# A chunked RWKV-7 scan on TensorE: products with a shared loaded side move 128 columns, k, b and v are turned by VectorE and GpSimd

## What is computed

```python
def rwkv7_scan(r, w, k, v, a, b):
    def step(state, inp):
        r_t, w_t, k_t, v_t, a_t, b_t = inp
        sa = jnp.einsum('bhvk,bhk->bhv', state, a_t)
        state = state * w_t[:, :, None, :] + sa[..., None] * b_t[:, :, None, :] + v_t[..., None] * k_t[:, :, None, :]
        return state, jnp.einsum('bhvk,bhk->bhv', state, r_t)
```

## Time and profile before

| | us |
|---|---|
| median of 3 runs | 2076.54 (2075.88 to 2079.14) |
| the profiled execution | 2082.89 |
| its span | 2081.1 |
| the scan in it, first to last matmul of L2650 | 734.8 to about 931.8 |

### The profile page before, as it was taken

The page is one execution under the profiler, slowest core; times in us unless marked ns, Lnnn a source line. Parts: engine busy times, 40 slices in busy tenths (PEclk is TensorE's granted clock), DMA queues, the critical chain, the costliest instruction groups (busy, mean ns, idle before and its releaser), DMA issues.

```text
span 2081.1 us, 34844 instructions
## 1 busy us (share of the span) xinstructions
PE 1975.6 (95%) x14762; PEld 1523.2 (73%) x14762; DVE 1091.2 (52%) x1727; ACT 802.3 (39%) x1363; POOL 378.3 (18%) x431
## 2 busy tenths in 40 slices
PE   8989999999999977669999999999999999999999
PEld 6847888888766666655887765468887778888887
DVE  4364444444667744437454765544455446666432
ACT  4264323232546522224324456654244442322211
POOL 0551000000303442212200036622221010000000
PEclk9999999999999999999999999999999999999999
DMA  5203333333342210001366210023332233333232
GB/s 184 78 26 96 91 101 91 91 94 98 102 152 73 81 44 4 5 6 67 96 167 216 70 33 1 1 93 101 91 115 80 70 95 97 91 92 96 89 94 86
DMA packets 46747, 174.87 MB, mean 84 GB/s; under 512 B 5072, under 2 KB 5584, under 8 KB 45825
## 3 DMA queue, kind: packets, MB, share of 16 engines
q1 hardware_dynamic: 43488, 154.09, 24.4%
q0 software_dynamic: 3104, 18.56, 2.7%
HBM read 166.26 MB, written 10.55 MB: 85 GB/s over the span
## 4 chain that ended last, share of the span: by engine, by line
PE 90%; issue 3%; DVE 3%; ACT 3%; POOL 0%; DMA 0%; SPq 0%; DVEq 0%; ACTq 0%; POOLq 0%
PE ps L300 22%; PE ps L301 22%; PE ps L305 22%; PE ps L2650 6%; PE ps L1425 2%; PE ps L1012 2%; PE ps L1409 1%; PE ps L1689 1%; ACT arena L1520 1%; PE ps L1378 1%; DVE arena L1481 1%; DVE arena L1465 1%; PE ps L1846 1%; PE ps L3228 1%; PE ps L2054 1%
## 5 line engine op out<-in xcount | busy, mean ns | idle before, releaser
L280 ACT ACTIVATE w_hi<-wring 128x1024 fp32r<-128x1024 f32 (+1 forms) x267 | 279.6, 1048 | 590.2 <-PE ps L305 568.1
L286 DVE TENSOR_TENSOR w_lo<-wring,w_hi 128x1024 fp32r<-128x1024 f32 (+1 forms) x267 | 330.8, 1239 | 229.6 <-ACT w_hi L280 228.2
L300 PE MATMUL ps<-ffn_input_hi,w_hi 128*128 128x512 f32 x352 | 139.7, 397 | 0.0
L301 PE MATMUL ps<-ffn_input_hi,w_lo 128*128 128x512 f32 x352 | 139.2, 395 | 0.0
L1567 POOL TENSOR_TENSOR arena<-arena 128x512 f32<-128x512 f32 (+3 forms) x160 | 111.3, 719 | 31.5 <-DVE arena L1473 26.5
L2650 PE MATMUL ps<-arena 64*64 64x64 f32 x3136 | 89.2, 226 | 28.4 <-issue 24.8
L300 PE MATMUL ps<-gate_input_hi,w_hi 128*128 128x512 f32 x256 | 106.3, 415 | 1.5 <-ACT gate_input_hi L829 1.5
L2650 PEld LDWEIGHTS ps<-arena 64*64 64x64 f32 x3136 | 81.6, 140 | 33.3 <-issue 28.7
L300 PE MATMUL ps<-mlp_input_hi,w_hi 128*128 128x512 f32 x256 | 101.7, 397 | 0.0
L300 PE MATMUL ps<-mlp_hi,w_hi 128*128 128x512 f32 x256 | 101.3, 396 | 0.0
L301 PE MATMUL ps<-gate_input_hi,w_lo 128*128 128x512 f32 x256 | 101.3, 396 | 0.0
(11 more groups left out here) (454 smaller groups left out, 4451.8 us busy)
## 6 DMA issues: line engine op xcount, KB each, us to landing
wring<-weights SPq DMA_DIRECT2D x276, 512.0 KB, 3.6
bias_wide_scratch<-bias_line_scratch POOLq DMA_DIRECT2D x1, 4096.0 KB, 24.6
arena<-bias_wide_scratch POOLq DMA_DIRECT2D x1, 4096.0 KB, 18.9
wring<-weights SPq DMA_DIRECT2D x8, 384.0 KB, 3.1
arena<-x_t SPq DMA_DIRECT2D x4, 512.0 KB, 7.6
xn_scratch<-arena POOLq DMA_DIRECT2D x1, 2048.0 KB, 7.4
x_scratch<-arena POOLq DMA_DIRECT2D x1, 2048.0 KB, 9.9
arena<-xn_scratch POOLq DMA_DIRECT2D x1, 2048.0 KB, 8.6
```

The costliest lines, as they stand in the source:

```text
L280: act.activation(self.w_hi[:, m % SPLIT, 0:n], self.wring[:, g % RING, 0:n], ACT.Copy).then_inc(self.w_hi_ready, 1)
L286: dve.tensor_tensor(self.w_lo[:, m % SPLIT, 0:n], self.wring[:, g % RING, 0:n], self.w_hi[:, m % SPLIT, 0:n].bitcast(F32), ALU.subtract).t ...
L300: pe.matmul(out, hi[:, c, :], src.hi[:, at + c, :], start=(at + c == 0), stop=False)
L301: pe.matmul(out, lo[:, c, :], src.hi[:, at + c, :], start=False, stop=False)
```

## The change

**Wide products.** Products that load the same matrix are made one, whose moving side is two matrices laid side by side (`twins`, L2713 of the new code): b with a and r (b0, b1), k with a and r (k0, k1), d2 with its transpose and me0 (t0, t1), d4 with its transpose and me1 (u0, u1). Each of their 16 matmuls moves 128 columns. The result fills two banks of four pairs each, and ScalarE copies both, in that order, into tiles that lie beside each other (`raw`, `d4t_me1`); the last, u, VectorE takes from PSUM itself.

**Turned blocks.** kt, bt and vt are no products any more. VectorE transposes the 32x32 blocks of a chunk of k, b or v into one buffer, `turned` (`turn`); ScalarE copies the buffer to kn, bn or vn (`settle`); GpSimd overwrites the blocks off the diagonal with four copies from the buffer, each 32 partitions of 8 x 32 (`swap`). The buffer is used again after that.

**Crossing.** With kt, bt and vt the half in which a head's rows lie changes: six products are now across where they were straight, or the other way about, and the pairs emitted in turns are others: y with rhs, y with m4, t with cross, u with sa. Others go alone.

**Masks.** rbt and rkt are masked by GpSimd from `raw`; dt, akt and me1 by VectorE from SBUF, no longer from PSUM.

The diff, cut; removed lines are in the listing above, and after the fourth line only added and kept ones are shown. Left out are the bookkeeping of semaphore counts, the places of the tiles, and the unchanged steps of VectorE.

```diff
-    PERIOD = (("next", "ba"), ("more", "kt"), ("now", "g"), ("more", "bt"), ("next", "d2"), ("next", "vt"),
-              ("now", "bonus"), ("now", "m4"), ("next", "d4"), ("now", "half"), ("next", "m1"), ("next", "ka"),
-              ("now", "cross"), ("next", "d8"), ("next", "kr"), ("now", "sa"), ("next", "m2"), ("next", "br"), ("next", "m3"))
+    FIRST = ("b0", "d2", "t0", "t1", "b1", "k0", "k1", "u0", "u1", "m3")
+    PERIOD = (("now", "g"), ("next", "b0"), ("next", "b1"), ("now", "m4"), ("now", "bonus"), ("next", "d2"), ("now", "half"),
+              ("next", "t0"), ("next", "t1"), ("now", "cross"), ("next", "k0"), ("next", "k1"), ("next", "u0"),
+              ("next", "u1"), ("now", "sa"), ("next", "m3"))
...
+    def turn(self, dve, name, c):
+        src = self.chunk({"k": self.prep.rkv[1], "b": self.prep.bb, "v": self.prep.rkv[2]}[name], c)
+        for before, at in self.token_at.items():
+            if at == self.token_at[name, c] - 1:
+                self.wait_shaped(dve, *before)
+        dve.transpose(self.buf["turned"], src).then_inc(self.turned, 1)
+    def settle(self, act, name, c):
+        self.wait_turned(act, name, c)
+        act.activation(self.in_tokens(name, c), self.buf["turned"], ACT.Copy).then_inc(self.copied, 1)
+    def swap(self, pool, name, c):
+        src, dst = self.buf["turned"], self.in_tokens(name, c)
+        pool.wait_ge(self.copied, self.token_at[name, c])
+        if self.shaped_at[name, c] > 1:
+            pool.wait_ge(self.shaped, self.shaped_at[name, c] - 1)
+        for e in range(2):
+            for i, j in ((0, 1), (1, 0)):
+                ins = pool.tensor_copy(dst[(2 * e + j) * 32:(2 * e + j + 1) * 32, :, i * 32:(i + 1) * 32],
+                                       src[(2 * e + i) * 32:(2 * e + i + 1) * 32, :, j * 32:(j + 1) * 32])
+        ins.then_inc(self.shaped, 1)
+        self.wait_shaped(pool, name, c)
...
+        def twice(p, out, lhs, rhs):
+            for h in range(2):
+                part = slice(h * HD, (h + 1) * HD)
+                mm = pe.matmul(out[part, p % 4], lhs[part, p, :], rhs(p)[part], start=True, stop=True)
             return mm
...
+        def twins(t, names, lhs, rhs, across=None, ready=None):
+            for half, name in enumerate(names):
+                k.open_aux(pe, t[name])
+                out = k.aux(t[name]).rearrange("p (a s b) -> p a s b", s=2, b=CH)
+                for p in range(4 * half, 4 * half + 4):
+                    if ready:
+                        ready(pe, p)
+                    mm = twice(p, out, lhs, rhs)
+                    if across and p == 7:
+                        mm.then_inc(k.aux_full, 1)
+                    if across:
+                        crossed = multiply(p, True, *across)
+                if not (across and half):
+                    mm.then_inc(k.aux_full, 1)
+            return crossed if across else None
...
             if now and c:
                 pe.wait_ge(self.state_ready, c)
                 k.open_acc(pe, t["y"])
                 _, whole = products(straight=(y, b["z"], rc, "first"), across=(rhs, ac, b["z"], "last"))
...
+                whole.then_inc(self.full, 1)
             if now:
...
+                self.wait_shaped(pe, "x32", c)
                 self.wait_turned(pe, "mn", c)
...
+                g, _ = products(straight=(aux(t["g"]), x32, b["mn"]))
                 g.then_inc(k.aux_full, 1)
...
+            if nxt and now:
+                twins(tn, ("b0", "b1"), bn_, ra_n)
...
             if now:
+                self.wait_shaped(pe, "v", c)
+                self.wait_shaped(pe, "rkt", c)
+                if not c:
+                    k.open_acc(pe, t["y"])
+                drained(t, "g", "m3")
+                _, m4 = products(straight=(y, vn, b["rkt"], "next" if c else "first"),
+                                 across=(aux(t["m4"]), b["gi"], b["me1"]))
+                m4.then_inc(k.aux_full, 1)
                 k.open_aux(pe, t["bonus"])
...
+                self.wait_shaped(pe, "rkk", c)
...
+            if nxt:
+                self.wait_turned(pe, "d", n)
+                d2, _ = products(straight=(aux(tn["d2"]), b["dt"], b["d"]))
+                d2.then_inc(k.aux_full, 1)
+            if now:
+                drained(t, "m4")
+                k.wait_acc_drained(pe, t["rhs"])
+                _, half = products(across=(aux(t["half"]), b["ml0"], b["rhs"]))
+                half.then_inc(k.aux_full, 1)
+            if more:
+                self.wait_shaped(pe, "k", c)
+                k.open_acc(pe, t["z"])
+                products(straight=(z, b["kn"], vn, "first"))
             if nxt:
                 drained(tn, "d2")
                 self.wait_turned(pe, "d2t", n)
...
+                self.wait_shaped(pe, "me0", n)
             if now:
                 drained(t, "half")
...
+                self.wait_shaped(pe, "x64", c)
+                if nxt:
+                    k.open_aux(pe, tn["t0"])
+                    k.open_aux(pe, tn["t1"])
+                crossing = (aux(t["cross"]), x64, b["half"])
+            if nxt:
+                cross = twins(tn, ("t0", "t1"), b["d2"], lambda p: b["d2t_me0"][:, :, p, :], across=crossing if now else None)
+            elif now:
+                _, cross = products(across=crossing)
+            if now:
                 cross.then_inc(k.aux_full, 1)
             if nxt:
...
+                twins(tn, ("k0", "k1"), kn_, ra_n)
+                self.wait_turned(pe, "me1", n)
+                self.wait_turned(pe, "d4", n)
             if now:
                 drained(t, "cross")
...
+                if nxt:
+                    k.open_aux(pe, tn["u0"])
+                    k.open_aux(pe, tn["u1"])
+                solving = (aux(t["sa"]), b["ml0"], b["rhs"])
+            if nxt:
+                sa = twins(tn, ("u0", "u1"), b["d4"], lambda p: b["d4t_me1"][:, :, p, :], across=solving if now else None)
+            elif now:
+                _, sa = products(across=solving)
+            if now:
                 sa.then_inc(k.aux_full, 1)
             if nxt:
...
+                self.wait_shaped(pe, "v", n)
+                self.wait_turned(pe, "akt", n)
                 k.open_acc(pe, tn["rhs"])
...
+                _, begun = products(across=(bank(k.acc(tn["rhs"])), b["akt"], b["vn"][n % 2], "first" if n else "whole"))
+                if not now:
+                    begun.then_inc(self.full, 1)
+            if more:
+                self.wait_shaped(pe, "b", c)
+                drained(t, "sa")
+                state, _ = products(straight=(z, b["bn"], b["sa"], "last"))
+                state.then_inc(self.full, 1)
             if nxt:
+                drained(tn, "u0", "u1")
+                m3, _ = products(straight=(aux(tn["m3"]), b["d8"], b["me1"]))
                 m3.then_inc(k.aux_full, 1)
             if now:
...
+                drained(t, "sa")
+                self.wait_shaped(pe, "rbt", c)
+                y_whole, _ = products(straight=(y, b["sa"], rbt, "last"))
+                y_whole.then_inc(self.full, 1)
...
+                self.wait_full(act, "rhs", c)
+                act.activation(b["rhs"], acc(t["rhs"]), ACT.Copy).then_inc(k.acc_drained[t["rhs"] % NA], 1)
             if nxt:
                 tn = self.t[n]
...
+                self.settle(act, "v", n)
+            if nxt and now:
+                self.wait_turned(act, "akt", c)
+                self.wait_shaped(act, "rkt", c)
+                copy_twins(tn, ("b0", "b1"), b["raw"])
...
             if now:
                 copy(t["m4"], b["ml0"])
             if nxt:
...
+                copy(tn["d2"], b["d2"])
             if now:
                 copy(t["half"], b["half"])
+            if more:
+                self.settle(act, "b", c)
             if nxt:
...
+                copy_twins(tn, ("t0", "t1"), b["d4t_me1"])
...
+                self.wait_shaped(act, "rbt", n)
+                copy_twins(tn, ("k0", "k1"), b["raw"])
             if now:
                 copy(t["sa"], b["sa"])
...
+                self.wait_full(act, "y", c)
                 act.activation(self.chunk(self.prep.rkv[0], c), acc(t["y"]), ACT.Copy).then_inc(
                     k.acc_drained[t["y"] % NA], 1)
+            if n < NCH - 1:
+                self.settle(act, "k", n)
...
+                tn = self.t[n]
+                if not now:
+                    self.prep.wait_shifted(dve, 16 + 7)
+                self.turn(dve, "v", n)
...
+                self.wait_shaped(dve, "me0", n)
+                k.wait_aux_drained(dve, tn["t0"])
+                k.wait_aux_drained(dve, tn["t1"])
+                dve.tensor_tensor(b["me1"], b["me0"], b["me1"], ALU.add).then_inc(self.turned, 1)
+                dve.transpose(b["d4"], b["d4t"]).then_inc(self.turned, 1)
+                k.wait_aux_drained(dve, tn["k0"])
+                k.wait_aux_drained(dve, tn["k1"])
```

(23 more changed lines are left out.)

247 lines of the change are left out of this document (91 added, 156 removed).

## The result

| | before | after |
|---|---|---|
| median of 4 runs, us | 2077.84 (2075.88 to 2080.96) | 2064.81 (2059.97 to 2066.79) |
| ratio, 95% interval | | 0.9928 (0.9908 to 0.9949) |
| profiled execution (its span) | 2082.89 (2081.1) | 2065.3 (2063.3) |

What follows compares the result with a forecast made beforehand. The scan was taken as bound by supply of TensorE's instructions, 23.95 us a period; after, waits for other engines give 21.65. Seven periods save 16.1 us, start and tail 0: 2076.5 to 2060.5 us, range 2046 to 2080.

Steps and rivals of the forecast that it cites:

- Supply of TensorE's instructions: Scan before: one block of 250 to 256 TensorE instructions each 3.81 us sets the pace, 24.0 us a period.
- gaps by time: Rival: TensorE's gaps in the scan go with time, not instructions; 24.1 us a period, 2077 us; chance 0.03.
- my three sections: One scan period walked from m3's end to d2, to u, to m3's end: 9.75 + 7.4 + 4.5 = 21.65 us.
- the GpSimd copy: Block copy of 32 partitions by 256 elements, 12 a period: 0.6 us each, four of k on the chain 2.4.
- The 20.4 us: Period estimated if GpSimd's one-input copies run near line rate, at 0.4 us each.
- The stall before d2: TensorE has 6.6 us of work while the chain to d2 takes 9.75, so it waits 3.1 us.
- The ports: VectorE and GpSimd operations both reading SBUF hold each other up; 0.9 us charged at the add to me1.
- The width: A 128-column matmul costs by its columns: 0.107 us a record pair, 1.71 us a product.
- Start and tail: Chunk 0's preparation and the last chunk's chain: both taken at 0, with 2 us either way.
- my case: Main forecast for the scan: 20.7 to 22.7 us a period, chance 0.46.
- the quick one: Rival: GpSimd copies of 0.35 to 0.45 us, little holding up; 19.5 to 20.3 us a period, 2048; chance 0.27.
- The circle on GpSimd: Rivals: GpSimd's own loop sets the period; no gain at 0.78 us a copy (0.13), slower from 0.80 (0.11).

Runs made afterwards that it cites:

- the filler: Changed kernel with 18 matmuls of 512 columns added after chunk 0's b0, in TensorE's wait ahead of d2: 2067.93 us, ratio 0.9938.
- the first group of experiments: Kernels run on one chip beside the kernel before (2079.74 us); the changed kernel, unaltered, ran again there: 2064.51 us, ratio 0.9924.

## Why the prediction was right, and where it wasn't

**The bound.** "Supply of TensorE's instructions" holds: 51 us of "issue" fell to 2.3 (I wrote under 10), whole-program packets from 118 to 104 (I wrote 13 fewer in the scan), and the added instructions cost 9 to 12 ns each before the change and 5 after. The rival "gaps by time" is out: the packets kept their pace when instructions were added.

**The period.** Forecast 21.65, measured 20.8 on average over all seven, 20.6 in the steady ones. By my three sections:

| section | forecast | measured |
|---|---|---|
| m3's end to d2 | 9.75 | 8.76 (857.65 to 866.41) |
| d2 to u | 7.4 | 7.18 (to 873.59) |
| u to m3's end | 4.5 | 4.69 (to 878.28) |

The first holds nearly all of the error. **The mis-sized term is the GpSimd copy:** 0.6 taken, 0.445 measured in the mean; k's four, which lie on the chain, take 1.70 and not 2.4, which is 0.7 of the 1.0. Grouped rows of 760 to 905 us:

```profile
L2667 POOL COPY arena<-root_in 32x256 f32<-32x256 f32 x64 | 28.5, 445 | 32.4 <-ACT arena L2657 29.5
L2967 DVE TENSOR_TENSOR arena<-arena,consts_sb 128x512 f32<-128x512 f32 x7 | 11.1, 1587 | 1.9 <-ACT arena L2866 1.9
...
L2963 DVE TENSOR_TENSOR arena<-arena 128x512 f32<-128x512 f32 x7 | 5.8, 826 | 0.0
```

The copy rows that I went by (1.8 ns an element) step over wider strides, which may be why they are slower (no run tests it); the memset of the earlier trace rows, which I took as a mere lower bound, gave 0.4 and was near. What the "GPSIMD Engine Reference" of the Trainium skill says in Engine selection, one-input operations at roughly line rate, agrees with 0.445. The 20.4 us that I put beside a copy of 0.4 doesn't come out of my own walk, though: only k's four copies stand in it, so 0.2 less for each gives 21.65 - 0.8 = 20.85, near the 20.8 measured.

**The stall before d2** was given as 3.1 us and is 1.24. One microsecond is the chain's, as above. The other 0.9 is TensorE's own side, 7.5 us and not 6.6: I counted the bonus as 0.43, where its four records need 0.86, the same slip as in the filler; from y's last matmul to the next product it is 0.96 where I had 0.7 (857.65 + 0.94 to 859.55), and the last record's tail of 0.2 wasn't counted. These slips don't change the sum, since that section goes by the other chain; they do raise the array's floor from 16.6 to 17.0.

**The ports.** Two operations that both read from SBUF do hold each other up at akt (L2967, 1.59 us; the state's L2989, of the same kind, takes 0.69), and GpSimd's L3025 takes 1.38 where it took 1.04. But in the place where I charged 0.9, the addition to me1 (L2963), it is 0.86 in the period shown, or 0.83 in the mean: 0.15. GpSimd stood in its copies of b there, which read one tile, not in a mask. In the version with b's copies first the same addition takes 1.08. Right in kind, on the path a sixth of the size. That section still came to 7.18, since 0.20 of "issue" and longer hand-overs filled part of it.

**The width.** 30 wide records take 1.64 us in the chain, so a pair steps by 0.109, where I took 0.107; a record is not as cheap as a narrow one (0.058).

**Start and tail** at 0, with 2 us either way: the tail was (0.26). The start lost 3.3, outside my bound. The step that failed is the sentence that takes chunk 0 at nothing. It names the turned blocks on that chain, and they cost 1.9 us; and it counts products, but not that they would run at half the clock, which costs 2.5 (I had read the clock in the middle alone). Before, the same low clock lay under the supply. The 1.0 us of the low clock in chunk 1's period wasn't in the sum either.

**The sum.** 7 x 2.3 = 16.1 was forecast; 22.19 - 3.32 + 0.26 = 19.1 in the traces and 13.0 between medians. That the time came out right is in part luck: two errors have opposite signs, the copy (some 5 us too dear, 7 x 0.7) and the start (3.3 too cheap), and 1.3 were lost behind the scan and 4.6 in the scatter of the profiled executions. Beside the kernel before in the first group of experiments the same kernel gained 15.2. **The rivals:** the measured period, 20.6 to 20.8, is at the low edge of my case (20.7 to 22.7), near the quick one, whose copy (0.35 to 0.45) is what the chip has. But quick copies alone didn't give 2048: the waits and the start kept the rest. The circle on GpSimd is there (the run with every copy made twice), and with copies of 0.88 us in effect the period is that of before; the program is longer, and the first mark comes 4.9 us later (758.77). I had the turning point at 0.80.

## What to carry over

Where an engine's gaps come at every 256 of its instructions and another engine's result never ends them, count its instructions: fewer and wider ones pay, and when they have paid, the next bound is whatever was hidden under the gaps, here a chain of copies through four engines. Then look for a copy that stands ahead of a more urgent one in an engine's queue; moving ScalarE's two copies of b ahead of one of v gave 7.0 us over the seven periods for no work. Time an operation by the row that reads and writes in the same pattern, and read the first instance of a loop for itself, with its own clock.

## What the hardware showed that I had not expected

- TensorE's granted clock fell to 0.50 in 4.5 us of idle time and stayed there until some 746.7 us, though there was work from 740.07 on; with matmuls in that idle time it stayed at 1.00, beside the same transfer, and fell at 758.1 instead. At the low level products bound by supply cost nothing that shows (247 records in 6.22 us without a gap); a lone narrow product (1.97 us against 0.95) and a wide one (3.40 against 1.96) nearly twice as much.
- An added two-column matmul, four instructions, costs 48 ns where the supply bounds (37 by the marks) and 21 where it doesn't.
- GpSimd copies 32 partitions x 256 elements in 0.39 to 0.41 us, what the memset on 128 partitions gives by its elements (an estimate of 0.43 from the earlier trace rows), so the four quarters in turn cost 1.70. With VectorE beside them the same four took 2.06.
